# Attention of a hybrid decoder layer: the softmax factor is multiplied into the probabilities on VectorE, the turn uses the identity, and ScalarE makes all copies

## What is computed

```python
p_c = softmax(where(ok_c, s_c, NEG)) * any(ok_c)[:, None]
o_c = einsum('bgrqk,bkgd->bgrqd', p_c, v_cmp)
...
p_s = softmax(where(dist_s >= 0, s_s, NEG))
o_s = einsum('bgrqk,bgqkd->bgrqd', p_s, v_g)
...
p_w = softmax(where(ok_w, s_w, NEG))
o_w = einsum('bgrqk,bkgd->bgrqd', p_w, v_w)
return gi[..., 0:1] * o_c + gi[..., 1:2] * o_s + gi[..., 2:3] * o_w
...
p = softmax(where(kpos <= t, s, NEG))        # MLA
o_mla = einsum('bhqk,bkhd->bqhd', p, v)
```

## Time and profile before

| | |
|---|---|
| median of three runs | 1728.08 us (1727.67 to 1728.74) |
| profiled execution | 1728.78 us, its span 1727.0 us |
| attention stage | about 145 to 320 us of the span |
| TensorE busy in it | 162.26 us |
| VectorE busy in it | 126.76 us |
| ScalarE busy in it | 89.35 us |
| GpSimd busy in it | 19.19 us |

### The profile page before, as it was taken

The page is one execution under the profiler, slowest core; times in us unless marked ns, Lnnn a source line. Parts: engine busy times, 40 slices in busy tenths (PEclk is TensorE's granted clock), DMA queues, the critical chain, the costliest instruction groups (busy, mean ns, idle before and its releaser), DMA issues. The chain is left out here.

```text
span 1727.0 us, 25483 instructions
## 1 busy us (share of the span) xinstructions
PE 1649.8 (96%) x8875; PEld 1332.3 (77%) x8875; DVE 1295.9 (75%) x3306; ACT 632.9 (37%) x1005; POOL 332.1 (19%) x305
## 2 busy tenths in 40 slices
PE   7999999889999999999979999997999999999997
PEld 5876767778865566667979999996888887888885
DVE  3457777445678797896787777885888887888887
ACT  3345545422210122123524445563333333333333
POOL 0100011101010354352023220002222222222220
PEclk9999999899999999999989999998999999999999
DMA  6530000322236799898678984437999999999995
GB/s 238 193 124 26 2 1 2 113 79 92 73 102 214 243 360 346 275 359 295 195 248 275 288 287 146 124 126 259 322 318 322 323 318 327 309 326 319 318 329 203
DMA packets 198270, 380.76 MB, mean 220 GB/s; under 512 B 16243, under 2 KB 130739, under 8 KB 197532
## 3 DMA queue, kind: packets, MB, share of 16 engines
q1 hardware_dynamic: 158832, 226.39, 39.6%
q0 software_dynamic: 37952, 143.18, 23.7%
q10 hardware_dynamic: 1388, 9.98, 1.4%
HBM read 340.66 MB, written 41.98 MB: 222 GB/s over the span
## 5 line engine op out<-in xcount | busy, mean ns | idle before, releaser
L1900 PE MATMUL psum<-v_hi,wa_hi 128*128 128x512 f32 x768 | 301.6, 393 | 13.7 <-DVE wa_lo L1850 13.7
L1900 PE MATMUL psum<-v_hi,wa_lo 128*128 128x512 f32 x768 | 300.9, 392 | 0.0
L1900 PE MATMUL psum<-v_lo,wa_hi 128*128 128x512 f32 x768 | 300.8, 392 | 0.0
L1809 ACT ACTIVATE v_hi<-v_raw 128x1024 fp32r<-128x1024 f32 x126 | 133.7, 1061 | 333.9 <-PE psum L1900 275.4
L1436 POOL DMA_INDIRECT u_rows<-u,eid x128 | 167.6, 1309 | 368.4 <-DVE sdot L1575 325.4
L1789 POOL DMA_INDIRECT v_rows<-v,eid x128 | 129.1, 1009 | 537.6 <-DVE x_back L1861 380.9
L103 PE MATMUL psum<-h_hi,u_hi 128*128 128x384 f32 x576 | 200.2, 348 | 13.0 <-DVE u_lo L1584 13.0
L103 PE MATMUL psum<-h_hi,u_lo 128*128 128x384 f32 x576 | 195.5, 339 | 0.0
L103 PE MATMUL psum<-h_lo,u_hi 128*128 128x384 f32 x576 | 195.4, 339 | 0.0
L1846 DVE TENSOR_TENSOR v_lo<-v_raw,v_hi 128x1024 fp32r<-128x1024 f32 x126 | 154.4, 1225 | 42.7 <-ACT v_hi L1809 41.1
L1900 PEld LDWEIGHTS psum<-v_hi,wa_hi 128*128 128x128 f32 x768 | 145.6, 190 | 45.1 <-DVE wa_lo L1850 9.4
(11 more groups left out here) (300 smaller groups left out, 2761.2 us busy)
## 6 DMA issues: line engine op xcount, KB each, us to landing
v_raw<-v SPq DMA_DIRECT2D x126, 512.0 KB, 5.4
u_raw<-uT SPq DMA_DIRECT2D x66, 512.0 KB, 4.9
v_first<-uT SPq DMA_DIRECT2D x62, 512.0 KB, 5.9
acts<-act_out SPq DMA_DIRECT2D x128, 192.0 KB, 3.0
acts_in<-acts SPq DMA_DIRECT2D x128, 192.0 KB, 5.5
wq_raw<-wq SPq DMA_DIRECT2D x16, 512.0 KB, 3.6
gates<-dense ACTq DMA_DIRECT2D x4, 2048.0 KB, 10.0
gates<-gates SPq DMA_DIRECT2D x31, 256.0 KB, 6.2
```

What stands on the lines that cost most here:

```text
L1809: act.activation(hi[:, c, :], raw[:, c, :], ACT.Copy).then_inc(vhi_ok, 1)
L1900: mm = pe.matmul(psum[:, 2 * t + b, :], w[:, c, ts], v[:, c, bs], start=(first and n == 0), stop=(last and n == 2), skip_group_check=True)
```

## The change

For units with b > 0, VectorE no longer writes a scaled identity; it multiplies the probabilities in place by the factor and the gate, over the unit's full width. TensorE turns them with a transpose against the plain identity, as it did for b = 0. All copies out of the turn banks go to ScalarE; `by_vector` and its semaphore `t_v` disappear, and with them VectorE's wait for the turn of u-4.

```diff
-        def by_vector(u):
-            return u % 4 in (0, 3)
         def copied(eng, u):
-            n = sum(by_vector(v) == by_vector(u) for v in range(u + 1))
-            eng.wait_ge(t_v if by_vector(u) else t_a, n)
+            eng.wait_ge(t_a, u + 1)
...
-            if by_vector(u):
-                nc.vector.tensor_copy(dst, src).then_inc(t_v, 1)
-            else:
-                nc.scalar.activation(dst, src, ACT.Copy).then_inc(t_a, 1)
+            act.activation(dst, src, ACT.Copy).then_inc(t_a, 1)
...
                 for n in range(4 if b == 0 else i + 1):
-                    if b == 0:
-                        mm = pe.transpose(psum[0:N_CMP, T_BANK + u % T_N, n * P:(n + 1) * P],
-                                          pr[:, u % RING, n * N_CMP:(n + 1) * N_CMP], m.eye[:, :])
-                    else:
-                        mm = pe.matmul(psum[:, T_BANK + u % T_N, n * P:(n + 1) * P],
-                                       pr[:, u % RING, n * P:(n + 1) * P], scale[:, u % RING, :], start=True, stop=True)
+                    w = N_CMP if b == 0 else P
+                    mm = pe.transpose(psum[0:w, T_BANK + u % T_N, n * P:(n + 1) * P],
+                                      pr[:, u % RING, n * w:(n + 1) * w], m.eye[:, :])
...
-                if TURN <= s < n_units + TURN and not by_vector(s - TURN):
+                if TURN <= s < n_units + TURN:
                     copy_out(act, s - TURN)
...
                 link(dve.reciprocal(fac[:, u, 0:1], sums[:, u, 0:1]))
-                if u >= RING:
-                    dve.wait_ge(t_mm, u - RING + 1)
-                dve.tensor_scalar(scale[:, u % RING, :], m.eye[:, :], fac[:, u, 0:1],
+                w = (i + 1) * P
+                dve.tensor_scalar(pr[:, u % RING, 0:w], pr[:, u % RING, 0:w], fac[:, u, 0:1],
                                   gate[:, b, h:h + 1] if b < 3 else None, ALU.mult, *([ALU.mult] if b < 3 else [])
                                   ).then_inc(d_ok, 1)
...
-                if TURN <= s < n_units + TURN and by_vector(s - TURN):
-                    copy_out(dve, s - TURN)
```

More of the change, by code:

```diff
@@ L677, in attend @@
         fac = sb("fac", [P, n_units, 4])
-        scale = sb("scale", [P, RING, P])
         og = sb("og", [P, 2, S])
@@ L683, in attend @@
         s_mm, s_in, e_ok, c_step, d_ok = sem("s_mm"), sem("s_in"), sem("e_ok"), sem("c_step"), sem("d_ok")
-        t_mm, t_v, t_a, v_mm = sem("t_mm"), sem("t_v"), sem("t_a"), sem("v_mm")
+        t_mm, t_a, v_mm = sem("t_mm"), sem("t_a"), sem("v_mm")
         og_ok, sq_ok, half_ok, ssq_ok, ohi_ok, olo_ok = (
@@ L700, in side, with copy_out @@
             return int(i >= QT // 2)
-        def by_vector(u):
-            return u % 4 in (0, 3)
         def copied(eng, u):
-            n = sum(by_vector(v) == by_vector(u) for v in range(u + 1))
-            eng.wait_ge(t_v if by_vector(u) else t_a, n)
-        def copy_out(eng, u):
+            eng.wait_ge(t_a, u + 1)
+        def copy_out(act, u):
             i, b, g = units[u]
-            eng.wait_ge(t_mm, u + 1)
+            act.wait_ge(t_mm, u + 1)
             if b == 0:
@@ L716, in copy_out @@
                 if u >= n_units // 2:
-                    eng.wait_ge(v_mm, valued(finish[1]))
+                    act.wait_ge(v_mm, valued(finish[1]))
             else:
@@ L722, in copy_out @@
                 if u >= RING and units[u - RING][1]:
-                    eng.wait_ge(v_mm, valued(u - RING))
+                    act.wait_ge(v_mm, valued(u - RING))
             src = psum[0:rows, T_BANK + u % T_N, 0:w]
-            if by_vector(u):
-                nc.vector.tensor_copy(dst, src).then_inc(t_v, 1)
-            else:
-                nc.scalar.activation(dst, src, ACT.Copy).then_inc(t_a, 1)
+            act.activation(dst, src, ACT.Copy).then_inc(t_a, 1)
         @block.sync
```

## The result

The changed kernel takes 1720.35 us (median; before 1727.92 us in the same comparison). The ratio is 0.9955 with an interval of 0.9941 to 0.9968: 7.6 us, or 0.45%, faster. The forecast was 1718.1 us in a range of 1706 to 1724. One of the 20 executions behind the median took 2074.9 us at a mean granted clock of 0.745; it stands outside the ratio, and the median of the other 19 is 1719.31 us. The profiled execution took 1723.73 us, with a span of 1722.0 against 1727.0.

What follows compares the result with a forecast made beforehand. TensorE bounded the attention stage before; after the change a loop through ScalarE's copies would. Gains of 0.6 and 9.4 us in the two halves sum to 10.0 us, giving 1718.1 us, range 1706 to 1724.

Steps and rivals of the forecast that it cites:

- Part 1: TensorE's 240 turns become transposes, one record each instead of two; TensorE sheds 30 us.
- Part 2: VectorE scales 128 to 512 columns in place, adding 9.6 us, and loses 52 copies, 25.95 us; ends at 110 us busy.
- The lower slope: VectorE's in-place scaling costs 67 ns per further 128 columns, rather than about 0.13 us as for copies and biases.
- Part 3: ScalarE takes all copies, 112 us busy; no bound by sum, but its fixed order closes a loop through three engines.
- the loop: Attention stage: turn, values, scores, bias, exponential, copy, exponential, copy, weight load; bounds each double period, gaining 0.6 and 9.4 us by half.
- double period: TensorE's unit of reckoning in attention: four units of head, branch and query tile; 12 non-compressed ones in either half.
- One sign: Next profile, ScalarE: its idle time would be ended by VectorE's bias more than by TensorE.
- The ceiling rival: TensorE stays the bound because the loop overlaps more than thought; gain near 30 us, 1698 us; chance 0.11.
- The clock rival: TensorE's idle time drops its clock to 1.2 GHz, losing 3.4 to 3.6 us per affected double period; 1745 us; chance 0.07.

Runs made afterwards that it cites:

- the two edits of the experiments: Changed kernel with ScalarE's copy of unit s-4 ahead of the exponential of unit s, and three PSUM banks for turns, two for outputs: 1699.49 us, ratio 0.9838.
- the third bank: Changed kernel with three PSUM banks for turns instead of two and two for outputs instead of three: 1714.91 us, ratio 0.9927.
- the shared copies: Changed kernel with `by_vector` restored, so VectorE makes 52 copies as before: 1717.20 us, ratio 0.9947.
- the extra transposes: Changed kernel with six extra, overwritten transposes before the turn of the first unit of each 128-wide pair: 1718.01 us, ratio 0.9950.
- two lines: Changed kernel with ScalarE's copy of unit s-4 moved ahead of the exponential of unit s: 1702.94 us, ratio 0.9859 to the kernel before.
- two other kernels: Changed kernel with three turn banks and two output banks, 1714.91 us; changed kernel with 52 copies back on VectorE, 1717.20 us.
- discarded work: Changed kernel with three products or six transposes, overwritten, before the first turn of each 128-wide pair: 1717.60 us with products, 1718.01 with transposes.

## Why the prediction was right, and where it was off

**Part 1 was right.** 240 records instead of 480. In the earlier trace rows the 16 records of a 512-wide pair lasted 2.05 us; the eight of now last 1.09.

**Part 2 was right in what it concluded, and 4 us off in its sum.** The lower slope held, 67 ns per 128 columns. VectorE is busy 114 us up to 315 us, where 110 was forecast. The copies' 25.95 us of rows were subtracted in full, but rows of neighbouring instructions overlap: taking the copies off alone took 20 us from VectorE's busy time. The load of VectorE did not matter: without its copies the kernel before became slower. ScalarE, forecast at 112 us, is busy 105 us up to 315 us.

**Part 3 and the loop were right to a few hundredths.** Forecast 5.82 and 6.18 us in the first half; undisturbed periods are 5.78 and, in the same trace, 6.14. Forecast 4.90 and 5.27 in the second; measured 4.92 to 4.97 and 5.28. This was not luck of offsetting errors; the steps of the loop came out one by one. From the start of the scores to the exponential it is 166.69 - 164.80 = 1.89 us, forecast 1.90; from there to the end of the second copy 169.18 - 166.69 = 2.49, forecast 2.49; then 0.14 to the turn, forecast 0.20; turn and values 1.26, forecast 1.23. For the branch b = 3 I took the gain of the others; it is 0.06 us per double period in the first half and 0.84 in the second. The whole is, in undisturbed periods, 12 x 0.08 + 12 x 0.78 = 10.3 us, forecast 10.0. Part 3 did not ask what the loop costs by being led through ScalarE: leaving VectorE its copies gives a double period of 5.57 us and some 3 us less in all. One sign did not come in the first trace: ScalarE waited longer for turns (27.6 us) than for the bias (21.7).

**The ceiling rival fell** for this kernel: 1698 us was not reached, because every period was bound by the loop. It came within 2 us once the two edits of the experiments opened the loop. So it was the loop, not TensorE's work, that was the bound.

**The clock rival came true in part.** I gave it 0.07 and treated it as all or nothing: a third of the double periods, and the time slower than before. What happened is a small dose in both traces of this kernel; the sign that was named for it, a clock under 0.9 over the stage, is met at its edge (0.89, or 0.90 up to 315 us). In the first trace the double periods of the first half add up to 6.2 us over their undisturbed length, so 10.3 - 6.2 = 4.1 us are left, against 5.0 us between the spans; the remaining 0.9 us I did not trace (both kernels also have falls at the stage's start and middle). In the medians 10.3 became 7.6; that the difference is the clock's is argued, not shown. The step that failed is the one that took the clock at 1.00 after 3.65 us of transposes for evidence that the clock would hold. It showed that transposes in an unbroken row hold it. It said nothing of a TensorE that is idle for a fifth of the time, which the earlier trace rows cannot show.

**The Trainium skill's rule**, TensorE: Matmul & The Clock Gate, Part 4: PE-mode transpose, that transposes do not engage the full clock, would have given some 1745 us. No run shows that: with all 240 transposes, the traces of the third bank, of the shared copies and of the extra transposes have a clock of 1.00 between 160 and 225 us. What makes the clock fall in the two traces of the changed kernel stays open. The transposes with 16% of idle time are not enough to make sure of a fall, since the traces of the third bank and of the shared copies have both and no fall there.

## What to carry to other kernels

When an engine in the middle of a loop does two kinds of work in a fixed order, put ahead the one whose input is ready and whose result is waited for: here two lines were worth more than twice the change itself. Measure the parts of a change apart: of the two made here, one gave 10 us and the other cost 3. Before forecasting a gain from less work on the bound engine, add up the longest loop through the buffers; the smaller of the two savings is the gain. An fp32 product with the identity costs two records of TensorE, a transpose one (480 against 240 here).

## What was not expected of the hardware

The granted clock fell to the lower level in the first half of the stage though TensorE's longest wait there was 0.89 us and it was busy for 55 of 65 us by the records. The kernel before, busy for 64.45 of 65 us, had no such fall. But two other kernels, busy for 55.51 and 56.70 us, had none either. Where the falls come differs from one execution to the next, and the same kernel spreads over 1714 to 1728 us. One trace is not enough to say that an edit cures a fall. About 0.7 us of discarded work per double period cost no time that these runs show.
